# Moving the activation tiles `h` and `hh` 32 bytes over in SBUF, by reordering allocations

## The reference, cut to what matters

```
h = modulate(x, norm_g[i, 0], mod[:, 0, 0], mod[:, 0, 1])
x = x + 0.5 * gate * ((silu(h @ w_gate) * (h @ w_up)) @ w_down)      # four of these, 2816 wide
...
proj = h @ w_in                                                       # SSD mixer, MLA mixer, two RWKV mixers
...
q = (h2 @ peer_q)                                                     # twice
act = gelu(einsum('td,ted->te', h2, u_sel)); einsum('te,ted->td', gate * act, v_sel)   # 16384 experts, twice
```

## Time and profile before

| | |
|---|---|
| median of 3 runs | 3390.74 us (3383.82 to 3403.28) |
| the profiled execution | 3383.82 us, of which the span of the trace is 3382.0 us |
| TensorE busy | 3244.8 us, 96% of the span |
| VectorE busy | 2580.9 us, 76% |
| ScalarE busy | 1609.0 us, 48% |
| mean granted TensorE clock | 0.987 |
| HBM read | 669.40 MB |

### The profile page before, as it was taken

How to read it: one execution, slowest core, us unless ns; L and a number is a source line. 1 busy time by engine, 2 the same in 40 slices (tenths; PEclk the granted TensorE clock), 3 DMA queues, 4 the chain that set the end, 5 groups by cost and what they waited for, 6 DMA issues and landing times.

```text
span 3382.0 us, 68787 instructions
## 1 busy us (share of the span) xinstructions
PE 3244.8 (96%) x26804; PEld 3102.4 (92%) x26804; DVE 2580.9 (76%) x4576; ACT 1609.0 (48%) x2594; POOL 197.1 (6%) x331
## 2 busy tenths in 40 slices
PE   6999989999999998999999999999899999999998
PEld 5999769999967997989999999998789999999998
DVE  7989667989836997747978777776846978877776
ACT  3456644454445445134455454445415445544444
POOL 1100001111100110200000000000300000000000
PEclk8999999999999999999999999999999999999999
DMA  9964218979613983045664576675115765567775
GB/s 374 382 227 167 74 44 330 388 285 389 267 38 111 401 310 119 18 162 185 227 204 172 172 238 232 231 233 172 69 49 180 237 226 181 173 211 235 238 232 181
DMA packets 246578, 707.46 MB, mean 209 GB/s; under 512 B 27472, under 2 KB 93008, under 8 KB 244928
## 3 DMA queue, kind: packets, MB, share of 16 engines
q1 hardware_dynamic: 212112, 571.64, 48.6%
q0 software_dynamic: 34224, 132.46, 10.2%
HBM read 669.40 MB, written 34.60 MB: 208 GB/s over the span
## 4 chain that ended last, share of the span: by engine, by line
PE 80%; DMA 7%; DVE 7%; ACT 3%; issue 2%; SPq 0%; DVEq 0%; POOL 0%; ACTq 0%; POOLq 0%
PE psum L515 34%; PE psum L548 26%; DMA ring<-stream 6%; PE psum L1072 3%; PE psum L894 2%; PE psum L1007 1%; DVE ring L1639 1%; PE psum L645 1%; ACT weights_hi L1144 1%; PE psum L914 1%; PE psum L496 1%; PE psum L527 1%; PE psum L528 1%; DVE arena L1697 1%; PE psum L729 1%
## 5 line engine op out<-in xcount | busy, mean ns | idle before, releaser
L515 PE MATMUL psum<-hh,weights_hi 128*128 128x256 f32 x4216 | 1187.2, 282 | 24.0 <-DVE ring L1639 10.4
L1144 ACT ACTIVATE weights_hi<-ring 128x1024 fp32r<-128x1024 f32 x711 | 752.9, 1059 | 949.9 <-DMA ring<-stream 895.2
L1639 DVE TENSOR_TENSOR ring<-ring,weights_hi 128x1024 fp32r<-128x1024 f32 x711 | 870.7, 1226 | 406.6 <-ACT weights_hi L1144 402.1
L515 PE MATMUL psum<-h,weights_hi 128*128 128x256 f32 x4216 | 1170.4, 278 | 0.0
L515 PE MATMUL psum<-hh,ring 128*128 128x256 f32 x2976 | 827.7, 278 | 0.0
L515 PEld LDWEIGHTS psum<-hh,weights_hi 128*128 128x128 f32 x4216 | 796.7, 189 | 33.0 <-DVE ring L1639 14.9
L515 PEld LDWEIGHTS psum<-h,weights_hi 128*128 128x128 f32 x4216 | 796.7, 189 | 0.2
L548 PE MATMUL psum<-small,weights_hi 128*128 128x256 f32 x2752 | 768.6, 279 | 3.0 <-DVE ring L1639 1.2
L548 PE MATMUL psum<-work,weights_hi 128*128 128x256 f32 x2752 | 765.4, 278 | 0.0
L548 PE MATMUL psum<-small,ring 128*128 128x256 f32 x2304 | 641.8, 279 | 0.0
L515 PEld LDWEIGHTS psum<-hh,ring 128*128 128x128 f32 x2976 | 563.9, 189 | 0.0
(11 more groups left out here) (410 smaller groups left out, 3894.6 us busy)
## 6 DMA issues: line engine op xcount, KB each, us to landing
ring<-stream SPq DMA_DIRECT2D x735, 512.0 KB, 3.9
arena<-mod_weights POOLq DMA_DIRECT2D x224, 512.0 KB, 7.0
arena<-stream SPq DMA_DIRECT2D x222, 512.0 KB, 6.6
acts<-small SPq DMA_DIRECT2D x256, 128.0 KB, 2.2
work<-acts SPq DMA_DIRECT2D x256, 128.0 KB, 3.1
arena<-cond_rows POOLq DMA_DIRECT2D x3, 1024.0 KB, 7.2
arena<-w_uq POOLq DMA_DIRECT2D x1, 3072.0 KB, 10.7
arena<-constants POOLq DMA_DIRECT2D x2, 1200.0 KB, 5.9
```

The costliest lines, as they stand in the source:

```text
L515: mm = pe.matmul(out, lhs[:, d, :], rhs[:, d, :], start=(d == 0 and p == 0), stop=(d == DT - 1 and p == 2))
L1144: act.activation(whi[:, NTH[n] % WS, :], raw(n), ACT.Copy).then_inc(sem["block_hi"], 1)
L1639: dve.tensor_tensor(low(n), raw(n), whi[:, NTH[n] % WS, :].bitcast(F32), ALU.subtract)\
```

## The change

No instruction changes. Two 8-byte pads are renamed, and one of them moves: it stands ahead of `x`, where it stood ahead of `h`. `h` and `hh` are allocated right after `x`, ahead of the small tables, where they came after them.

```diff
-        sb("ahead_of_weights", [P, 2])
+        sb("line_half", [P, 2])
         ring, (ring_lo,) = sb_twice("ring", [P, RING, 1024], [([P, RING, 1024], F32R)])
...
         sb("arena_high", [P, 128 - 30 - 4 * MORE, 256])
+        sb("line_rest", [P, 2])
         x = sb("x", [P, DT, T])
+
+        h, (h_lo,) = sb_twice("h", [P, DT, T], [([P, DT, T], F32R)])
+        hh, (h_hi,) = sb_twice("hh", [P, DT, T], [([P, DT, T], F32R)])
         vfirst = sb("vfirst", [P, 4, T])
         cols = sb("cols", [P, NCOLS])
...
         omk = sb("one_minus_k_a", [P, 8])
-        sb("ahead_of_activations", [P, 2])
-        h, (h_lo,) = sb_twice("h", [P, DT, T], [([P, DT, T], F32R)])
-        hh, (h_hi,) = sb_twice("hh", [P, DT, T], [([P, DT, T], F32R)])
+
         work, (_, gat_lo) = sb_twice("work", [P, 2048], [([P, 1024], F32), ([P, 4, T], F32R)])
```

## The result

The kernel became slower: 3418.1 us (median of 8, 3411.9 to 3425.5) against 3386.6 us before (median of 8, 3382.1 to 3403.3), a ratio of 1.0085 with an interval of 1.0069 to 1.010. The profiled execution took 3425.5 us with a span of 3423.6 us, 41.6 us more than the profiled one of before; the mean granted clock was 0.988 against 0.987, so the clock has no part in it.

What follows compares the result with a forecast made beforehand. TensorE, busy 96% of the span, was taken as the bound. Gains of 14.5 (FFN), 6.2 (SSD, MLA, RWKV), 3.1 (`peer_q`) and 21.1 us (`u`) made 45: 3383.8 to 3339, or 3345 against the median; range 3302 to 3415.

Steps and rivals of the forecast that it cites:

- One reading fits all three: Float32r streams take 4 bytes a cycle in 64-byte pieces; an aligned start of `h`, `hh` needs 16, not 17: 256 cycles, not 272.
- The price of 109 ns: Pace expected for matmuls with `h` or `hh` moving, from 113.3 ns: 4.3 ns less, times 13368, 57.5 us before other limits.
- The bound by L1007: Plain float32 matmul's pass of 256 columns, 108.8 ns with a full weight load, taken as the next limit for L515.
- Rival 2: Moving and stationary streams of the 13368 matmuls meet: 6.7 ns each, 89 us more, 3480; chance 0.20 with its milder form.
- the milder form: All 13368 matmuls at L548's slow pace, 117.8 ns: 4.5 ns each, 60 us more, 3450; within the 0.20 for slower.
- Its sign, 117 to 120 ns in the chain: A long run of L515 in the chain after, divided by its count, would show 117 to 120 ns if the streams meet.
- the aligned stream needs one piece less: Argument against the streams meeting: `h` and `hh`, starting at a multiple of 64, need 16 pieces of 64 bytes, not 17.
- Rival 1: Nothing changes: the 16 cycles belong to every float32r matmul or go by 128 bytes; L515 stays at 113.3 ns, 3390; chance 0.18.
- The share that passes on: Part of the matmul gain reaching the kernel time: 80% in FFN gate and up (14.5 us) and in `u` (21.1 us).
- No cost elsewhere: L548 keeps its pace, and moving `kept`, `zeros`, `x`, `cols`, `modc` costs 0, with 5 us either way as the bound.
- (288 + 288 + 272) / 3: L548's slow stretches at 117.8 ns read as two of three matmuls paying 16 cycles: 282.7 cycles on average.

Runs made afterwards that it cites:

- m4_starts: Kernel of matmuls alone, ten pairs of places (d: weights 160, moving 96), each begun ten times: distance 112 272 cycles in 40 of 40 starts, 192 in 39 of 40.
- m1_places: Kernel of matmuls alone, 48 for each of 64 pairs of moving and stationary places, 0 to 224 modulo 256 in steps of 32: 410.5 us; gives the table of all pairs.
- f1_h_at_96: Against the changed kernel, `h` and `hh` 32 bytes further in the new order; `h`, `hh`, `work`, `small` at 224 modulo 256, distance 64: 3435.8 us, ratio 1.0109 to before.

## Why the prediction was wrong

- **"One reading fits all three"** is the step that failed. It took the 16 cycles above 256 as a 17th piece of 64 bytes that an aligned start saves. Multiples of 64 run at 272 at best (32-column loads at 192; weights at 0 with `h` at 192). The step went from two places of the moving operand, 272 and 288 cycles, to a rule about that operand, and forecast 109 ns where 116.7 came, though between the two its distance to the weights had changed as well. Their distances, 192 and 0, have these two paces in the table of all pairs.
- **The price of 109 ns** hung on it. The bound by L1007 was right as a measure of plain float32 (259 cycles a pass, 107.9 ns, wherever it begins), and says nothing of float32r.
- **Rival 2 was right,** at a chance of 0.20: the two streams meet. The runs show that the pace goes by their distance; that they meet in the memory is an inference. It named the distance, with the modulus 128 where it is 256, and took 288 cycles or 282.7. Distance 32 gave 280 to 282.7, so 3.2 ns a matmul and 43 us, where the milder form said 4.5 ns and 60. Its sign, 117 to 120 ns in the chain, was near (116.7). Its argument against, "the aligned stream needs one piece less", was the failed reading again.
- **Rival 1's** weight rested on the same row. The Trainium skill (SBUF — State Buffer, section Who interferes with whom) gives TensorE two independent read ports, one for the moving operand and one for the weight load, and says that it never waits on anyone. The runs disagree: with the distance of the two reads the pace goes from 272 to 288 cycles, at the full clock and with 256 columns.
- **The share that passes on** was put at 80% for a gain. TensorE's slowing by the change passed on nearly whole, 43 us of matmuls to 41.6 us of span; at distance 96 some 70% of it did, 88 us to 64. The prediction had no number for a loss. The gain of distance 112 passed on in part, 14 us of 22 if the medians are taken.
- **No cost elsewhere** was right: L548's mean pace didn't rise, the tables moved for nothing (ratio 1.000), and no wait appeared. No run shows at what rate a plain float32 pass needs its bytes; what they show is that it takes 259 cycles at four places, and that `kept` and `zeros` cost nothing at 32.

What stays open: what in the memory makes two reads 32 bytes apart worse than 192 or 112, why a float32r stream takes 17/16 of its columns at the full clock even with a short load, and what decides between 272 and 282.7 cycles at distances 192 and 64. The prediction read 282.7 as (288 + 288 + 272) / 3, two of three matmuls paying 16 cycles. The traces speak against that: in the slow start of pair d in `m4_starts` every interval behind the first three is 117 to 119 ns, none is 113 or 120.

## What to carry to other kernels

Where a float32r matmul with a full weight load bounds a kernel, measure the pace by pairs of addresses, not by one operand's: sweep the distance between the starts of moving and stationary operand (over 256 bytes here) in a kernel of a few hundred microseconds, with several starts and several pairs for each distance, since one distance can have two paces. Moving a tensor for the sake of alignment changes its distance to everything that is read beside it. And before one rule is read out of two rows, list everything that differs between them.

## What the runs showed of the hardware

- float32r, 128x128 by 128x256, at the full clock: 272 cycles at distance 112 in all of 41 bursts. At 192 it is 272 or 282.7: 3 of 8 pairs in `m1_places`, 39 of 40 starts in `m4_starts`. The other distances tried modulo 256 took 277 to 304 (the table above has those in steps of 32), but for two stretches at 272 cycles at distance 64 in `f1_h_at_96`.
- At the half clock the same instruction took 256 cycles of 1.2 GHz (213.3 ns), at distance 224, where the full clock gives 284 of 2.4 GHz (118 ns).
- Floors for 256 columns: float32r 272, one element read 256 times 268, bf16 262, a plain float32 pass 259. The weight load alone takes 268. The Trainium skill (TensorE: Matmul & The Clock Gate, section Back-to-back issue gap) has 262; bf16 here agrees, float32r is 10 cycles above it.
- Distance 192 has two paces that each last for a whole burst or stage, 272 and 282.7 cycles. At distance 112 no stretch at 282.7 was seen, the kernel is faster (ratio 0.9942), and its nine executions lie within 12 us, the eleven of its control within 25.
